# A transformer block pair on one core: the second modulation's weighted sums move from TensorE to ScalarE, GpSimd and VectorE

## What is computed

```
mod_x = silu(c) @ w_ada + b_ada            # 6 x 1024 columns
mod_c = silu(c_ctx) @ w_ada + b_ada
sh_a, sc_a, g_a, sh_m, sc_m, g_m = split(mod_x, 6)
hx = rmsnorm(x) * (1 + sc_a) + sh_a        # mod_c the same for the context's 256 tokens
qa, ka, va, qb, kb, vb, ga, gb = split(hx @ w_in)
x  = x + g_a * merge(attention_a, attention_b, sigmoid gates)
h  = rmsnorm(x) * (1 + sc_m) + sh_m
x  = x + g_m * moe(h)                      # 32 experts, top 4 of each token
... a second block: three attentions, then a squared-relu MLP, final norm
```

## Time and profile before

| | us |
|---|---|
| time, median of 3 runs | 1780.64 (1779.58 to 1781.3) |
| the profiled execution's own time | 1779.28 |
| its span | 1777.5 |
| PE busy | 1649.6 (93%) |
| VectorE busy | 695.5 (39%) |
| ScalarE busy | 286.3 (16%) |
| GpSimd busy | 25.1 (1%) |

### The profile page before, as it was taken

The page is one execution under the profiler, slowest core; times in us unless marked ns, Lnnn a source line. Parts: engine busy times, 40 slices in busy tenths (PEclk is TensorE's granted clock), DMA queues, the critical chain, the costliest instruction groups (busy, mean ns, idle before and its releaser), DMA issues.

```text
span 1777.5 us, 19026 instructions
## 1 busy us (share of the span) xinstructions
PE 1649.6 (93%) x7320; PEld 889.1 (50%) x7320; DVE 695.5 (39%) x1272; ACT 286.3 (16%) x623; POOL 25.1 (1%) x30
## 2 busy tenths in 40 slices
PE   5999999999989898898898988998999999999998
PEld 3556786534333242332332423332686778888743
DVE  2453432332323223232232232332134663677755
ACT  3123450301010010000100101000243334010000
POOL 0210000000000000000000000000000000000000
PEclk9999999999999999999999999999999999999999
DMA  9796225799999999999999999999524333444440
GB/s 381 270 321 194 95 98 202 293 426 429 430 430 430 430 430 428 430 430 430 429 430 430 429 430 430 430 429 418 209 97 142 115 123 143 142 170 163 156 175 24
DMA packets 85535, 537.20 MB, mean 302 GB/s; under 512 B 6081, under 2 KB 7489, under 8 KB 59873
## 3 DMA queue, kind: packets, MB, share of 16 engines
q1 hardware_dynamic: 81664, 530.60, 73.6%
q10 hardware_dynamic: 3808, 5.78, 0.9%
HBM read 535.31 MB, written 1.05 MB: 302 GB/s over the span
## 4 chain that ended last, share of the span: by engine, by line
PE 72%; DMA 25%; DVE 1%; ACT 1%; issue 1%; DVEq 0%; ACTq 0%; SPq 0%; POOL 0%; POOLq 0%
PE ps L1854 23%; PE ps L2216 21%; DMA ring<-in_w_up 12%; DMA ring<-in_w_gate 10%; PE ps L2527 6%; PE ps L2715 5%; PE ps L2196 3%; PE ps L2286 2%; DMA arena<-in_w_down 2%; DMA ring<-in_w_ada 1%; PE ps L1965 1%; PE ps L2628 1%; PE ps L1880 1%; PE ps L2077 1%; PE ps L1993 1%
## 5 line engine op out<-in xcount | busy, mean ns | idle before, releaser
L2216 PE MATMUL ps<-ring,arena 128*64 128x512 f32 x2288 | 512.3, 596 | 57.1 <-DMA ring<-in_w_gate 28.3
L2216 PEld LDWEIGHTS ps<-ring,arena 128*64 128x64 f32 x2288 | 160.8, 137 | 389.6 <-issue 313.7
L1854 PE MATMUL ps<-arena,ring 128*128 128x256 f32 x896 | 199.9, 381 | 0.3 <-ACT arena L749 0.3
L2216 PE MATMUL ps<-arena 128*64 128x512 f32 x784 | 178.9, 602 | 10.1 <-DMA arena<-in_w_up 5.4
L1854 PEld LDWEIGHTS ps<-arena,ring 128*128 128x128 f32 x896 | 168.6, 190 | 33.4 <-issue 7.3
L1854 PE MATMUL ps<-ring,arena 128*128 128x512 f32 (+1 forms) x480 | 162.9, 495 | 1.3 <-ACT arena L867 1.3
L822 ACT ACTIVATE arena<-ps 128x512 f32<-128x512 f32 x32 | 19.1, 597 | 671.3 <-PE ps L2257 671.3
L1854 PEld LDWEIGHTS ps<-ring,arena 128*128 128x128 f32 x480 | 90.2, 190 | 66.6 <-issue 59.2
L2216 PEld LDWEIGHTS ps<-arena 128*64 128x64 f32 x784 | 56.0, 138 | 118.7 <-issue 102.1
L1378 DVE TENSOR_TENSOR arena<-ps,arena 128x512 f32<-128x512 f32 x32 | 22.1, 692 | 201.9 <-PE ps L2216 201.9
L1403 DVE TENSOR_TENSOR arena<-ps,g_moe 64x512 f32<-64x512 f32 x32 | 21.9, 683 | 187.2 <-PE ps L2216 187.2
(11 more groups left out here) (332 smaller groups left out, 1539.5 us busy)
## 6 DMA issues: line engine op xcount, KB each, us to landing
ring<-in_w_up SPq DMA_DIRECT2D x55, 2048.0 KB, 33.8
ring<-in_w_down SPq DMA_DIRECT2D x55, 2048.0 KB, 32.1
ring<-in_w_gate SPq DMA_DIRECT2D x49, 2048.0 KB, 33.6
ring<-in_w_in SPq DMA_DIRECT2D x23, 2048.0 KB, 8.1
arena<-in_w_up SPq DMA_DIRECT2D x17, 2048.0 KB, 31.3
arena<-in_w_down SPq DMA_DIRECT2D x17, 2048.0 KB, 32.0
arena<-in_w_gate SPq DMA_DIRECT2D x15, 2048.0 KB, 30.8
ring<-in_w_ada SPq DMA_DIRECT2D x12, 2048.0 KB, 16.7
```

Source lines behind the costliest of these rows:

```text
L1854: last = pe.matmul(dst, a, b, start=k == 0, stop=k == len(terms) - 1)
L2216: mm = pe.matmul(dst[CAP * g:CAP * g + CAP, :], stationary(half, c), w[:, c, 512 * g:512 * g + 512], start=half == 0 and c == 0, stop=half ...
```

## The change

Each chunk's products and the sum over the eight chunks are made off PE, for c alone. ScalarE multiplies chunks 0 to 3 of block n in place in the ring by silu(c) of the partition (`ada_products`, in its steps 4 to 11). GpSimd adds these four up with three adds (`ada_half`), one block in each of its turns u = 5 to 11 behind the power of that turn, and the last block behind the turns. VectorE adds chunks 4 to 7 with four multiply-adds (`ada_rest`), one block in each turn u = 5 to 11 behind `hat` and `modulation_out`, ahead of the token sums, and the last one behind the loop. PE only sums over the partitions with a column of ones (`mod_sums`). `modulation_out(n)` moves from turn n + 4 to turn n + 3.

```diff
+            def ada_half(n):
+
+                acc, w = ada_sum[:, n % 2, :], wq_view(W_ADA2[n - 4])
+                pool.wait_ge(sem("modp_done"), part(n))
+                if n >= 6:
+                    pool.wait_ge(sem("modt_done"), part(n - 2))
+                for j in range(1, 4):
+                    last = pool.tensor_tensor(acc, acc if j > 1 else w[:, 0, :], w[:, j, :], ALU.add)
+                    if j < 3:
+                        pool.drain()
+                last.then_inc(sem("ada_half"), 1)
+
             for u in range(12):
                 inverse_root(nh_rs[:, 0:2 if u < 4 else 8])
+                if u >= 5:
+                    ada_half(u - 1)
+            ada_half(11)
...
+            def ada_products(n):
+
+                i = W_ADA2[n - 4]
+                act.wait_ge(loaded[i % RING], 16 * (i // RING + 1))
+                w = wq_view(i)
+                for j in range(4):
+                    last = act.activation(w[:, j, :], w[:, j, :], ACT.Copy, scale=cs_t[:, j, 0:1])
+                last.then_inc(sem("modp_done"), 1)
+
             for s in range(15):
-                if ada_step(s) is not None:
-                    modulation(ada_step(s))
...
+                if 4 <= s < 12:
+                    ada_products(s)
...
-                dve.tensor_reduce(modT[:, 4 * n:4 * n + 4, :],
-                                  bank(mod_bank(n)).rearrange("p (q g m) -> p q g m", q=4, g=4)[:, :, :, 0:2]
-                                  .rearrange("p q g m -> p q m g"), AX.X, ALU.add).then_inc(sem("modt_read"), 1)
+                dve.tensor_copy(modT[:, 4 * n:4 * n + 4, 0], bank(mod_bank(n), 4)).then_inc(sem("modt_read"), 1)
+
+            def ada_rest(n):
+
+                w, acc = wq_view(W_ADA2[n - 4]), ada_sum[:, n % 2, :]
+                dve.wait_ge(sem("ada_half"), n - 3)
+                for j in range(4, KC):
+                    last = dve.scalar_tensor_tensor(acc, w[:, j, :], cs_t[:, j, 0:1], acc, ALU.mult, ALU.add)
+                    if j < KC - 1:
+                        dve.drain()
+                last.then_inc(sem("ada_done"), 1)
...
-                if u == 8:
+                if u == 7:
                     dve.wait_ge(sem("small_in"), 64)
-                if ada_step(u) is not None:
-                    modulation_out(ada_step(u))
+                if u >= 7:
+                    modulation_out(u - 3)
+                if u >= 5:
+                    ada_rest(u - 1)
...
-            modulation_out(8)
+            ada_rest(11)
             modulation_out(9)
...
-            def ada(n, i):
-                ready(i)
-                if n > 4:
-                    pe.wait_ge(sem("modp_done"), part(n - 1))
-                w = wq_view(i)
-                for c in range(2):
-                    for g in range(4):
-                        last = pe.matmul(bank(ada_bank(n))[32 * g:32 * g + 32, :], cs_t[:, 2 * g + c, :],
-                                         w[:, 2 * g + c, :], start=c == 0, stop=c == 1)
-                        tell_used(last)
-                last.then_inc(sem("ada_done"), 1)
-                used()
...
+            def mod_sums(n):
+
+                pe.wait_ge(sem("ada_done"), part(n))
                 if n > 4:
                     pe.wait_ge(sem("modt_read"), part(n - 1))
+                src, dst = ada_sum[:, n % 2, :], bank(mod_bank(n))
+                if 6 <= n < 10:
+                    for q in range(4):
+                        last = pe.matmul(dst[:, q:q + 1], src[:, q:512:4] if n in (6, 7) else src[:, P * q:P * q + P], one,
+                                         start=True, stop=True)
+                        if q == 0:
+                            tell_used(last)
+                else:
+                    for q in range(2):
+                        last = pe.matmul(dst[:, T * q:T * q + T], one.broadcast_to([P, P]), src[:, T * q:T * q + T],
+                                         start=True, stop=True)
+                        if q == 0:
+                            tell_used(last)
                 last.then_inc(sem("modt_done"), 1)
+                used()
...
             for s in range(15):
                 if ada_step(s) is not None:
-                    ada(ada_step(s), W_ADA2[ada_step(s) - 4])
+                    mod_sums(ada_step(s))
...
-                if ada_step(s) is not None:
-                    (mod_transpose if 6 <= ada_step(s) < 10 else mod_rows)(ada_step(s))
...
-            ada(11, W_ADA2[7])
...
-            mod_rows(11)
+            mod_sums(11)
```

More of the change, by code:

```diff
@@ L215, in part @@
             return n - 2 if n else 1
-        def ada_bank(n):
-            return 6 if n else 0
         def mod_bank(n):
             return 2 if n == 0 else 7 if n < 11 else 5
+        ada_sum = modp2
+        one = stat[:, 54:55]
         cs_t = rw_t[:, :].rearrange("p (j m) -> p j m", j=KC)
@@ L629, in _ @@
             act.dma_start(row[:, :], t["row"].broadcast_to([P, N_ROW])).then_inc(sem("row_in"), 16)
[L631 to L638, removed]
+            act.wait_ge(sem("ada_done"), 1)
+            act.activation(modp[:, 0, :], bank(0), ACT.Copy).then_inc(sem("modp_done"), 1)
             act.dma_start(const[:, P:C_ROPEC], t["const"][:, P:C_ROPEC]).then_inc(sem("const_in"), 16)
@@ L695, in _ @@
                     qk_out(s - 3)
-            modulation(11)
+                if 4 <= s < 12:
+                    ada_products(s)
+            act.wait_ge(sem("ada_done"), part(11))
             act.dma_start(rw_t[:, :], t["router_w"]).then_inc(sem("rw_in"), 16)
@@ L1047, in _ @@
             dve.memset(cs_t, 0.0)
+            dve.memset(one, 1.0)
             dve.drain()
@@ L1089, in add_bias @@
             def add_bias(c0, n):
-                dve.tensor_tensor(modT[:, c0:c0 + n, :], modT[:, c0:c0 + n, :],
-                                  vec[:, V_BADA + c0:V_BADA + c0 + n].unsqueeze(2).broadcast_to([P, n, 2]), ALU.add)
+                dve.tensor_tensor(modT[:, c0:c0 + n, 0], modT[:, c0:c0 + n, 0], vec[:, V_BADA + c0:V_BADA + c0 + n], ALU.add)
                 dve.drain()
@@ L1204, in _ @@
             add_bias(32, 8)
-            dve.tensor_tensor(modT[:, 24:32, :], modT[:, 24:32, :], bshift.unsqueeze(2).broadcast_to([P, KC, 2]), ALU.add)
+            dve.tensor_tensor(modT[:, 24:32, 0], modT[:, 24:32, 0], bshift, ALU.add)
             dve.scalar_tensor_tensor(scale_m[:, :], modT[:, 32:40, 0], 1.0, vec[:, V_NM:V_NM + KC],
@@ L1886, in mod_transpose @@
             def mod_transpose(n):
                 pe.wait_ge(sem("modp_done"), part(n))
+                for q in range(4):
+                    last = pe.transpose(bank(2)[:, P * q:P * q + P], modp[:, 0, P * q:P * q + P], ident)
+                last.then_inc(sem("modt_done"), 1)
+            def mod_sums(n):
+                pe.wait_ge(sem("ada_done"), part(n))
                 if n > 4:
                     pe.wait_ge(sem("modt_read"), part(n - 1))
-                src = (modp2 if n else modp)[:, n % 2, :]
@@ L1891, in mod_transpose @@
-                for q in range(4):
-                    last = pe.transpose(bank(mod_bank(n))[:, P * q:P * q + P],
-                                        src[:, q:512:4] if n in (6, 7) else src[:, P * q:P * q + P], ident)
-                last.then_inc(sem("modt_done"), 1)
-            def mod_rows(n):
-                pe.wait_ge(sem("modp_done"), part(n))
-                if n > 4:
-                    pe.wait_ge(sem("modt_read"), part(n - 1))
-                else:
-                    pe.wait_ge(sem("row_in"), 32)
-                pe.matmul(bank(mod_bank(n)), const[:, C_ROW0:C_ROW0 + 1].broadcast_to([P, P]), modp2[:, n % 2, :],
-                          start=True, stop=True).then_inc(sem("modt_done"), 1)
+                src, dst = ada_sum[:, n % 2, :], bank(mod_bank(n))
```

## The result

The changed kernel takes 1803.43 us (median of 4 runs, 1802.58 to 1806.35) against 1780.11 of the kernel before beside it: a ratio of 1.0139 [1.0127, 1.0152], 23.3 us more. The prediction was 1799.6 us, with slower at 0.83. The profiled execution took 1803.49 us, its span 1801.7 us, 24.2 more than before.

The account below looks back on a forecast made before the run. PE's work bounds the stage; the change makes a VectorE-GpSimd round trip the bound. `values` group 21.3 us later, 4.2 less PE work, 3.2 for the clock: +20.3 on 1779.28 gives 1799.6 us, range 1787 to 1815.

Parts of the forecast that it names:

- The adds, h = 4.3, 1.4 each: GpSimd's three adds per turn: 1.4 us each, twice VectorE's 0.69, with two drains 4.3 us; ends 2.2 and 8.6.
- A turn, 11.0: VectorE-GpSimd round trip: 3.4 to the power's end, 4.3 adds, 3.3 multiply-adds, 11.0 us against PE's step of 8.4.
- Turn 5 begins at 66.15: VectorE's turn 5 was to start at 66.15 us as before, with nothing new ahead of it.
- Seven turns, 77.0: VectorE's turns 5 to 11 at 11.0 us each were to take 77.0 us, before token sums and `vb_sums`.
- Group 21.3 later: PE's second group of `values` in step 13, begun at 131.41 us before, was to begin 21.3 us later.
- PE's work behind it, -4.2: From that `values` group to the first scores, PE was to have 4.2 us less work.
- `mod_sums` with one moving column, 0.94 each: PE's four products with one moving column, eight records, were to take 0.94 us per block, 3.8 for four blocks.
- rival 1: The gain arrives: GpSimd's adds about 0.5 us, turns fit PE's step, 12.7 us come off, 1766.6 us; chance 0.10.
- The clock, +3.2: Behind PE's last wait, in step 13, a fallen clock was to add 3.2 us.
- One for one to the end: A shift of PE at 150 us was to pass unchanged through attention and experts to the kernel's end.
- Rivals 2 and 4: GpSimd's adds cost 0.69 us each, total 1781.7, chance 0.07; or 2.8 us each, total 1830, chance 0.05.
- Rival 3: GpSimd's first add starts behind VectorE's embedding and `hat` instructions, costing 7.4 us: 1807.0 us; chance 0.12.

Follow-up runs that it names:

- the last experiment: Kernel before the change, VectorE summing chunks 3 to 7, first three blocks' sums inside turns 5 to 7, modulation reads a turn earlier: 1774.95 us, ratio 0.9973.

## Why the prediction was right

The mechanism was the one named: a round trip of VectorE and GpSimd per turn, longer than PE's step, with PE held to it. By its own terms:

- **Start to end of the power, 3.4.** Measured 3.36 (103.29 to 106.65).
- **The adds, h = 4.3, 1.4 each.** Measured 4.6 with embedding: 1.53 for the first, which begins beside the last embedding product (L1165), 1.53 for the second, beside `hat`, and 1.28 for the third. The third add of turn 6, with VectorE idle, took 1.26. The ends of 0.69 and 2.8 were far off on both sides. That the middle of two such distant ends came within 0.3 is in part luck: no row stood for it, and its 0.14 above the 1.26 covered some of a hold-up that the text had put at nothing. The estimate of 1.12 us in proportion, from the 4497 ns for 2048 elements in the Trainium skill, "GPSIMD Engine Reference", section 3.1, was below the 1.26.
- **The multiply-adds, 3.3.** Measured 3.23 and the hand-over: 3.36.
- **A turn, 11.0.** Measured 11.31 in turns 5, 8, 9 and 10. In turns 6 and 7, which have no embedding, 10.7 and 10.9: there the power took 1.64 and the first add 1.26.
- **Turn 5 begins at 66.15.** It began at 64.52: PE left its first half-clock stretch earlier (16 products in 5.20 us, not 6.75). Another start, not another cost, and not the change's doing: see the last experiment.
- **Seven turns, 77.0.** Measured 80.8, and this is the step that was short: 0.3 for each of the five turns with embedding, and 2.7 in turn 11 on top, less 0.4 in turns 6 and 7. There GpSimd goes on at once with the last block's adds, beside VectorE's multiply-adds; the text took these to run at their own pace (3.3). In the run that kept them apart they took 3.22.
- **Group 21.3 later.** 23.7, that is -1.6 for the start and +3.8 for the turns, and 0.2 of rounding and token sums.
- **PE's work behind it, -4.2.** As said; the wait for the sums of quarters (0.61) wasn't in the text.
- **`mod_sums` with one moving column, 0.94 each.** True for n = 8 and 9 (1.09 and 1.02 for the eight records), but n = 6 and 7 took 2.00 and 1.92, at a granted clock of 1.00. They differ in that each loads every fourth column of the sum as weights. So PE's step is some 9.2 us there and not 8.4, and the net of 12.7 us was some 1.9 too large. A turn of 11.3 us covered it; it would have come off the gain of rival 1.
- **ScalarE, 2.2 a block.** Measured 2.56, and covered as said.
- **The clock, +3.2.** 2.2. Half of 9.38 us was run at the lower level (the window of 156 to 158 us shows 0.50, that of 160 to 162 us 1.00), not the whole of a group as in the earlier trace rows.
- **One for one to the end.** True up to the experts (22.26), and 1.9 on top near 1260 us that no step had, 1.1 of it the pause that goes with the changed code.

Together that is 22.3 in the stage where the text had 20.3. The text's places for the waits also held: L1920 at 88 to 98 (86.3 to 98.2), L1986 at 142 to 152 (143.9 to 155.1), VectorE 2 to 4 us ahead of L1121 (1.96 to 2.58), and no wait for ScalarE's L692. VectorE's turns were 10.7 to 11.3 us apart, token sums aside, but the last took 13.95.

**The rivals.** The gain would have needed adds of 0.5 us. The run with one add, so with an h of 1.5, had turns of 8.7 to 9.2 us, where the text's arithmetic gives 8.2, with VectorE's own instructions filling them. Rival 1's bound of h = 1.9 missed this, since it left out `modulation_out` and a stretched `hat`. Rivals 2 and 4 fell with the adds' length. Rival 3 named a real mechanism and had its size nearly right, though not its form: the first add does not start behind VectorE's instructions, it and the second take 0.27 us more when they start beside one. Three adds at 1.26 with two gaps of 0.14 would be 4.06; they took 4.6 with embedding and 4.3 without. That is 0.56 us in five turns and 0.28 in two, some 3.4, and with the 2.66 of turn 11 some 6 us of the 7.4 foreseen. VectorE loses more (0.84 of `hat` in each turn), but in time in which it would have waited for the adds anyway. The forecast held against this rival only because its own adds of 1.4 stood above the 1.26. The rule of the Trainium skill, "SBUF — State Buffer", "Who interferes with whom", agrees with these rows for adds of 512 elements a partition. It would have given the missing term of turn 11, had it been applied to every pair of neighbours and not only to `hat`.

## What to carry to other kernels

Work that leaves the busiest engine for two others which hand it to each other costs the whole round trip, not the busier of the two: write the chain of one turn and compare it with the step it must fit in, before looking at busy shares. GpSimd beside VectorE is no free third engine: here seven multiply-adds on VectorE alone were faster by 8 us than four with GpSimd's help. And where a helper engine has a short read that the main engine waits for, put it ahead of the long new work and put that work into gaps; the same arithmetic gave nothing at first and 0.27% after two such moves. And before two traces are compared at a late point, compare them at a point ahead of the change: here PE was up to 3.0 us ahead there.

## What the runs showed of the hardware

- VectorE's operations of 128 x 512 on two SBUF inputs take up to 1.76 us instead of 0.69 while GpSimd adds tiles of that size, and four multiply-adds up to 5.89 instead of 3.23. GpSimd's add takes 1.26 with VectorE idle and 1.53 at most.
- VectorE's `TENSOR_SCALAR` on 128 x 8, in SBUF with one tensor input, took 1.08 us beside them instead of 0.17 (L1047 above). So not only instructions with two tensor inputs are held.
- GpSimd's power of 128 x 8 is hardly touched by VectorE's embedding beside it: 1.75 us, against 1.64 without.
- An add of 128 x 512 takes GpSimd 1.26 us and a power of 128 x 8, with 64 times fewer elements, 1.64. The power of 128 x 2 took 0.70, so six more elements cost 0.94: most of the 1.64 goes with the number of elements, and the powers say nothing of how fast GpSimd adds.
- Four products with one moving column took PE 1.92 us when their weights were every fourth column of a tile, and 1.02 when they were 128 neighbouring columns, both at a granted clock of 1.00 (120.39 and 142.85 us in the changed kernel). The mean weight load was 0.33 against 0.19 us.
